# Second block: one run of 24 projection tiles with the spatial gating issued between them

## What is computed

```python
def spatial_gating(u, v, norm_w, ws, bs):
    v = rms_norm(v, norm_w).reshape(B, S // GM_CHUNK, GM_CHUNK, GM_HEADS, GM_HEAD_DIM)
    w = jnp.where(causal, ws, 0.0)
    s = jnp.einsum('hts,bnshd->bnthd', w, v) + bs.T[:, :, None]
    return u * s.reshape(B, S, GM_WIDTH)

def hybrid_mixer(p, ...):                  # p = h @ w_in
    uv = jax.nn.gelu(p[..., COL_GM:COL_Q])
    y_a = spatial_gating(uv[..., :GM_WIDTH], uv[..., GM_WIDTH:], gm_norm_w, gm_ws, gm_bs)
    qkv = jax.nn.silu(short_conv(p[..., COL_Q:COL_Z], conv_w))
    ...                                    # q, k, v, and z = p[..., COL_Z:COL_A]
    o = gated_delta_rule(q, k, v, g, beta)
    y_b = rms_norm(o, o_norm_w) * jax.nn.silu(z)
    return jnp.concatenate([y_a, y_b], axis=-1)
```

## Time and profile before

| | us |
|---|---|
| median of 3 runs | 4131.07 |
| the three runs | 4123.65, 4131.07, 4134.15 |
| span of the profiled execution | 4134.1 |
| gm tiles, from the first matmul | 48.6 |
| gating, no projection tile | 40.3 |
| qkv tiles | 71.7 |
| between qkv and z | 7.0 |
| z tiles | 23.8 |

### The profile page before, as it was taken

The page is one execution under the profiler, slowest core; times in us unless marked ns, Lnnn a source line. Parts: engine busy times, 40 slices in busy tenths (PEclk is TensorE's granted clock), DMA queues, the critical chain, the costliest instruction groups (busy, mean ns, idle before and its releaser), DMA issues. The chain is left out here.

```text
span 4134.1 us, 50723 instructions
## 1 busy us (share of the span) xinstructions
PE 3717.7 (90%) x19009; PEld 3217.5 (78%) x19009; DVE 2578.6 (62%) x4191; ACT 1165.2 (28%) x2042; POOL 338.4 (8%) x281
## 2 busy tenths in 40 slices
PE   8998988899977897989999979999988889689998
PEld 7877755687855796789999979999967758567876
DVE  4556666544645465388999867777754437655544
ACT  1100133211031332133678843333321123412200
POOL 0000010000000020003212322222100000000000
PEclk9999999999989798999999989999999989889999
DMA  4334201232522001158989889999822111022232
GB/s 151 99 105 173 82 11 36 95 95 66 206 75 82 1 1 56 56 176 283 312 290 319 319 310 317 322 320 335 281 82 87 64 36 48 1 82 76 86 107 76
DMA packets 199980, 591.06 MB, mean 143 GB/s; under 512 B 22240, under 2 KB 80480, under 8 KB 197856
## 3 DMA queue, kind: packets, MB, share of 16 engines
q1 hardware_dynamic: 162928, 454.34, 32.8%
q0 software_dynamic: 36864, 134.23, 9.1%
HBM read 536.07 MB, written 52.43 MB: 142 GB/s over the span
## 5 line engine op out<-in xcount | busy, mean ns | idle before, releaser
L615 DVE CAST w_hi<-w_ring 128x1024 fp32r<-128x1024 f32 (+1 forms) x336 | 238.1, 709 | 449.6 <-PE banks L569 402.3
L71 DVE TENSOR_TENSOR w_lo<-w_ring,w_hi 128x1024 fp32r<-128x1024 f32 (+1 forms) x336 | 424.5, 1263 | 11.6
L2753 PE MATMUL out_ps<-w_hi,v_hi 128*128 128x384 f32 x1024 | 349.4, 341 | 41.8 <-DVE w_lo L71 41.8
L569 PE MATMUL banks<-x_hi,w_hi 128*128 128x512 f32 x896 | 355.7, 397 | 29.1 <-DVE x_lo L71 29.1
L2453 PE MATMUL up_ps<-h_hi,u_hi 128*128 128x384 f32 x1024 | 351.2, 343 | 20.2 <-DVE u_lo L71 20.1
L569 PE MATMUL banks<-x_lo,w_hi 128*128 128x512 f32 x896 | 354.3, 395 | 0.0
L569 PE MATMUL banks<-x_hi,w_lo 128*128 128x512 f32 x896 | 353.9, 395 | 0.0
L2753 PE MATMUL out_ps<-w_hi,v_lo 128*128 128x384 f32 x1024 | 347.3, 339 | 0.0
L2753 PE MATMUL out_ps<-w_lo,v_hi 128*128 128x384 f32 x1024 | 347.2, 339 | 0.0
L2453 PE MATMUL up_ps<-h_lo,u_hi 128*128 128x384 f32 x1024 | 343.9, 336 | 0.0
L2453 PE MATMUL up_ps<-h_hi,u_lo 128*128 128x384 f32 x1024 | 343.6, 336 | 0.0
(11 more groups left out here) (563 smaller groups left out, 7705.1 us busy)
## 6 DMA issues: line engine op xcount, KB each, us to landing
expert_tiles<-peer_u SPq DMA_DIRECT2D x128, 512.0 KB, 5.0
expert_tiles<-peer_v SPq DMA_DIRECT2D x128, 512.0 KB, 5.4
w_ring<-w_in SPq DMA_DIRECT2D x104, 512.0 KB, 3.7
w_ring<-ffn_up SPq DMA_DIRECT2D x88, 512.0 KB, 3.6
w_ring<-w_ff SPq DMA_DIRECT2D x64, 512.0 KB, 3.7
ada_ring<-w_ada SPq DMA_DIRECT2D x48, 512.0 KB, 6.4
peer_acts<-act_ring SPq DMA_DIRECT2D x128, 192.0 KB, 5.4
peer_gates<-staging SPq DMA_DIRECT2D x12, 2048.0 KB, 11.1
```

What stands on the lines that cost most here:

```text
L71: return nc.vector.tensor_tensor(self.lo[at], value, self.hi[at].bitcast(F32), ALU.subtract)
L569: last = nc.tensor.matmul(banks[:, j, s, 0:n], a[:, u % 2, k, :], b[:, g * kg + k, x_from + c:x_from + c + n], start=(g == 0 and k == 0 an ...
L615: nc.vector.tensor_copy(w_parts.hi[:, u % 2], ring[:, u % slots]).then_inc(hi_ready, 1)
L2753: last = nc.tensor.matmul(out_ps[:, b, P:T], a[:, n % 2, b * P:b * P + P], r[:, n % 2, :], start=(n == 0 and part == 0), stop=(n == NKEYS ...
```

## The change

A new helper `projections` replaces the three calls of `linear` by one unrolled run of 24 tiles in one block: the same ring, the same split, the same 24 matmuls for a tile, four banks. After each tile it calls `pe_beside`, which puts other TensorE work between tiles; `act_out` and `dve_out` are told the tile's number and put in the gating's ScalarE and VectorE work. The tiles now come in the order v, u, qkv, z (numbers 0 to 3, 4 to 7, 8 to 19, 20 to 23). The four banks that `projections` leaves are one tile `side`, which the front-end norms, the norm of v, the transposes and the mixing matmuls share.

```diff
+def projections(p, x, w, spans, lot, act_out, dve_out, stages, also, banks=None, pe_beside=None):
...
+        @block.tensor
+        def _(pe):
+            for stage in front:
+                stage.tensor(pe)
+            for n in range(nb):
+                pe.wait_ge(w_ready, n + 1)
+                if n >= lot:
+                    pe.wait_ge(bank_free[n % lot], n // lot)
...
+                last.then_inc(units_done, 1)
+                if pe_beside is not None:
+                    pe_beside(pe, n)
...
+            def split(n):
+                dve.wait_ge(landed[n % RING], 16 * (n // RING + 1))
+                if n >= 2:
+                    dve.wait_ge(units_done, n - 1)
...
+            for n in range(nb):
+                if 1 < n + 1 < nb and n:
+                    split(n + 1)
+                dve_out(dve, n, n % lot, psum(n), bank_free[n % lot], units_done)
...
-                linear(p, "gm", d["w_in2"][0:8], DB, 8, h_parts, act_out=copy_out(p, uv, ACT.Gelu_apprx_tanh),
-                       stages=normed_tokens)
...
-                    run(p, [Landed(landed, len(tables)), Norm(p, c3, v, v, 4, T, RMS_EPS, gm_norm, center=False)])
-                spatial_gating(p, uv, mix, v_rows, wT, causal, bs)
...
-                    linear(p, "qkv", d["w_in2"][8:20], DB, 12, h_parts, also={RING - 1: fetch_z},
-                           **short_conv(p, c3, qkv, conv_w, T))
-
-            linear(p, "z", d["w_in2"][20:24], DB, 4, h_parts, act_out=copy_out(p, z, ACT.Silu), before=project_qkv)
...
+        def pe_beside(pe, n):
+            if n == U[0]:
+                for b in range(4):
+                    pe.wait_ge(squared, b + 1)
+                    last = nc.tensor.matmul(side[:, 0, :], p.ones, squares[:, b, :], start=(b == 0), stop=(b == 3))
+                last.then_inc(summed, 1)
+            if n == U[2]:
+                pe.wait_ge(rooted, 1)
+                for b in range(4):
+                    pe.wait_ge(v_scaled, b + 1)
+                    for c in range(NC):
+                        last = nc.tensor.transpose(side[:, b, c * P:c * P + P], v[:, b, c * P:c * P + P], p.ident)
+                    last.then_inc(turned, 1)
+            if n in range(Z[0] - 1, Z[3]):
+                b = n - Z[0] + 1
+                pe.wait_ge(rows_taken, 4)
+                if b >= 2:
+                    pe.wait_ge(biased, 2 * (b - 1))
                 for j in range(2):
+                    for c in range(NC):
+                        last = nc.tensor.matmul(side[:, 2 * (b % 2) + j, c * P:c * P + P], v_rows[:, c, b, :], wT[:, 2 * b + j, :],
+                                                start=True, stop=True)
+                    last.then_inc(mixed, 1)
+
+        def act_out(act, n, j, psum, bank_free):
...
+            if n == V[3]:
+                for b in range(4):
+                    nc.scalar.activation(squares[:, b, :], v[:, b, :], ACT.Square).then_inc(squared, 1)
+            if n == U[0]:
+                act.wait_ge(prepared, 2)
+                act.wait_ge(summed, 1)
+                nc.scalar.activation(rstd[:], side[:, 0, :], ACT.Sqrt, bias=eps_col[:], scale=1.0 / (4 * P)).then_inc(rooted, 1)
+            if n == U[3]:
+                for b in range(4):
+                    act.wait_ge(turned, b + 1)
+                    nc.scalar.activation(v_rows[:, :, b, :], side[:, b, :].rearrange("p (c n) -> p c n", n=P), ACT.Copy) \
+                        .then_inc(rows_taken, 1)
+            if n in QKV:
+                conv.scalar(act, n - QKV[0], psum, bank_free)
...
+        def dve_out(dve, n, j, psum, bank_free, units_done):
...
+            if n == U[0]:
+                dve.wait_ge(rooted, 1)
+                nc.vector.reciprocal(rstd[:], rstd[:]).then_inc(inverted, 1)
+            if n == U[1]:
+                dve.wait_ge(inverted, 1)
+                for b in range(4):
+                    nc.vector.scalar_tensor_tensor(out=v[:, b, :], in0=v[:, b, :], scalar=gm_norm[:, b:b + 1], in1=rstd[:],
+                                                   op0=ALU.mult, op1=ALU.mult).then_inc(v_scaled, 1)
+            if n in QKV:
+                conv.vector(dve, n - QKV[0])
+            if n in Z:
...
+        projections(p, h_parts, d["w_in2"], [(0, T)] * 24, 4, act_out, dve_out, normed_tokens, {}, pe_beside=pe_beside)
```

More of the change, by code:

```diff
@@ L199, in __init__ @@
     def __init__(self, p, ctx, src, dst, kb, width, eps, gain, bias=None, center=True, func=ACT.Identity,
-                 parts=None, first=0, after=None, squares=None, rstd=None, root_in_bank=False, tally=None, lo_ready=None, lo_from=0):
+                 parts=None, first=0, after=None, squares=None, rstd=None, root_in_bank=False, tally=None, lo_ready=None, lo_from=0, sums=None):
         self.p, self.src, self.kb, self.width, self.eps = p, src, kb, width, eps
@@ L211, in __init__ @@
         self.eps_col = p.sb(ctx, "eps_col", [P, 1])
[L212 removed]
+        self.sums = p.ps(ctx, "sums", [P, 2 if center else 1, halves, 512])[:] if sums is None else sums
         if root_in_bank:
@@ L1556, in spatial_gating @@
     with ExitStack() as ctx:
+        h_parts = Parts(p, ctx, "h", [P, DB, T])
+        uv = p.sb(ctx, "uv", [P, 8, T])
         v = uv[:, 4:8, :]
[L1558 to L1571 removed]
+        v_rows = p.sb(ctx, "v_rows", [P, NC, 4, P])
@@ new lines, in project_and_gate @@
+        squares = v_rows[:].rearrange("p c b n -> p (c b n)").rearrange("p (b t) -> p b t", t=T)
+        wT = p.sb(ctx, "wT", [P, GM_HEADS, P])
+        bs = p.sb(ctx, "bs", [P, 4, P])
+        rstd = p.sb(ctx, "v_rstd", [P, T])
+        eps_col = p.sb(ctx, "v_eps", [P, 1])
+        side = p.ps(ctx, "side", [P, 4, T])
+        evicted, prepared, squared, summed, rooted, inverted, v_scaled, turned, rows_taken, mixed, biased, gated = p.sems(
+            ctx, "evicted", "prepared", "squared", "summed", "rooted", "inverted", "v_scaled", "turned", "rows_taken", "mixed",
+            "biased", "gated")
@@ new lines, in project_and_gate, with normed_tokens @@
+        conv = ShortConv(p, ctx, qkv, conv_w, T)
+        tables = (*mixer_tables, (wT[:], d["gm_ws"]), (bs[:], d["gm_bs"]))
+        def normed_tokens(c, banks):
+            for to, source in tables:
+                nc.sync.dma_start(to, source).then_inc(landed, 16)
+            done = Norm(p, c, x, x, DB, T, BETA_LN_EPS / ALPHA ** 2, ln3[:, 0, :], ln3[:, 1, :], tally=sum3,
+                        squares=uv[:, 0:4, :], rstd=rstd[:], sums=side[:, 0:2, :].unsqueeze(2))
+            return [done, Norm(p, c, x, h, DB, T, RMS_EPS, gain, shift, center=False, parts=h_parts, after=done,
+                               squares=uv[:, 4:8, :], sums=side[:, 2:3, :].unsqueeze(2))]
@@ L1579, in _ @@
-            dve.wait_ge(gated, n)
-        @block.tensor
-        def _(pe):
-            pe.wait_ge(masked, 1)
-            for b in range(4):
-                for j in range(2):
-                    for c in range(NC):
-                        last = nc.tensor.matmul(banks[:, j, b, c, :], v_rows[:, c, b, :], wT[:, 2 * b + j, :],
-                                                start=True, stop=True)
-                    last.then_inc(summed, 1)
+                    nc.vector.tensor_tensor(out, side[rows, 2 * (b % 2) + j, :].rearrange("p (c t) -> p c t", t=P),
+                                            over(bs[rows, b:b + 1, :], [64, NC, P]), ALU.add).then_inc(biased, 1)
```

137 lines of the change are left out of this document (96 added, 41 removed).

## The result

The changed kernel took 4090.97 us (median of 4 runs, 4088.87 to 4092.02), the kernel before 4130.74 (4 runs, 4123.65 to 4134.15): a ratio of 0.9901, 95% interval 0.9887 to 0.9915, or 39.8 us less. The forecast was 4092.3.

What follows compares the result with a forecast made beforehand. Program order alone was taken to put the gating on TensorE's path. Removing 142.8 us and putting back 89.8 for tiles and 14.2 for side work saves 38.8: 4131.07 - 38.8 = 4092.3 us, range 4083 to 4105.

Steps and rivals of the forecast that it cites:

- What bounds: Mixer's projections and gating: only program order puts the gating, 40.3 us with TensorE busy for 15.9, on the path.
- The loop: Qkv projection: register addresses make looped tiles take 5.92 us, against 5.62 where the round is written out.
- My bound of 3.6: Upper bound for qkv: 12 tiles at the loop's pace, 0.30 us more each, 3.6 us more in all.
- Rival 1: Qkv stays at 5.92 us a tile because fetches slow it; 3.6 us more, 4095.9 us; chance 0.11.
- The tiles: Projections after the change: twelve qkv tiles 67.4 us and four z tiles 22.4, together 89.8.
- The work between tiles: Gating work on TensorE's path: sums 3.4, stall 1.94, transposes 1.8, mixing 7.0; 14.2 us with a small restart.
- stall: Before tile 6, TensorE waits 1.94 us for the weight split queued on VectorE behind the norm's reciprocal.
- The sum: Whole stage: 142.8 us removed, 89.8 and 14.2 put back, 38.8 us saved; profiled execution 4095.3, median 4092.3.
- rival 2: TensorE's clock drops behind tile 6's stall or in the mixing; 1.8 to 5.1 us more, about 4096; chance 0.13.
- Rivals 3 and 4: Rival 3, and a rival where the low clock holds: 4.7 us more a tile, 4167 us; chance 0.02.
- rival 3: Inserted gating work makes TensorE wait for other engines; half of 24.4 idle us returns, about 4104.5; chance 0.04.
- The test of the other stages: Sign against the forecast: the sum is wrong if another stage of the kernel moves by more than a microsecond.

Runs made afterwards that it cites:

- qkv_unrolled: Kernel before with only the three rounds of the qkv projection loop written out; 4127.70 us, ratio 0.9985 to the kernel before.
- no_gating: Changed kernel with the whole gating left out and half of the mixer's output set to one; 4080.68 us, ratio 0.9861 to the kernel before.
- gating_together: Changed kernel, still one run of 24 tiles, but with the whole gating behind tile 7; 4106.90 us, ratio 0.9925 to the kernel before.
- again: Changed kernel run once more with no edit, to see the spread; 4092.55 us, ratio 0.9887 to the kernel before.
- banks_first: Changed kernel with the four projection PSUM banks allocated ahead of the gating's tile; 4086.62 us, ratio 0.9882 to the kernel before.
- pad32: Changed kernel with 32 bytes left empty ahead of the split weights of the 24 tiles; 4093.03 us, ratio 0.9884 to the kernel before.
- transposes_thrice: Changed kernel with each of the 16 transposes behind tile 6 issued three times; 4102.15 us in one run.

## Why the prediction was right, point by point

**What bounds.** TensorE's order bounded the stage and nothing else took its place: with the gating out of the way TensorE is busy for 67.80 of 67.80 us in the qkv tiles and 29.58 of 29.60 in z. A small wait hides in the busy time: in qkv every second tile comes 0.07 us late.

**The loop.** I read 5.92 against 5.62 as register addresses. `qkv_unrolled` shows it by itself, as the price of the loop: 5.61 a tile, 2.5 us over the qkv tiles. My bound of 3.6 charged all 12 tiles, but only the first 8 are in the loop. Rival 1 falls.

**The tiles.** Forecast 67.4 for qkv and 22.4 for z. Measured 5.62 + 62.18 = 67.8 and 29.60 less four mixings. In `no_gating` tiles lie 5.62 apart (first to last copy of z, 1330.10 to 1346.95, three steps). The term was 0.5 short: 0.4 from every second qkv tile at 5.69 where I had 5.62 for all, and 0.1 from z at 5.62 where I had 5.60.

**The work between tiles.** Forecast 14.2, measured 14.2 with and without the gating. By parts, each against 5.62: sums 9.04 - 5.62 = 3.42 (3.4); stall 7.59 - 5.62 = 1.97 (1.94), of which the hole shows as 1.71; transposes 7.38 - 5.62 = 1.76 (1.8); mixing 4 x 1.78 = 7.1 (7.0). The stall's good fit is luck in part, for two misses cancel in it: split and hand-overs took 1.86 us from the reciprocal's end to TensorE's start where I had 2.09, so the hole is 0.23 shorter than my 1.94, and the start behind the hole costs 0.26 besides where I had 0.1. The lower ends, taken from warm rows, were right in each case where the rows gave two ends.

**The sum.** 191.4 - 153.3 = 38.1 against 38.8. Of the 0.7, 0.5 are the tiles', 0.1 the side work's and 0.1 the first eight tiles', 48.74 (1208.83 to 1264.72 less 3.42, 1.97 and 1.76) against 48.6. That the median of the whole kernel came within 1.3 us of the forecast (4090.97, 4092.3) is luck in part: the profiled execution missed its forecast by 5.1 (4090.2, 4095.3), for reasons outside the stage (below).

**The clock (rival 2).** It stayed at 1.00 after the hole of 1.71 us and through the transposes. The mechanism is real, as the hole of 4.95 us shows, but this stall didn't set it off, and neither did the same hole in the five other kernels that have it (1.69 to 1.74). Of the holes between, the kernel before has one of 1.79 us that kept the clock and one of 3.06, which the prediction left out of its list, behind which the mixing starts at the lower level; its window there:

```profile
1275.20:1278.00 2.80, 2.79 (x13) 2.79 (x14) 0.68 (x1) 0.00 (x0) 0.00 (x0) 0.50 0.00 0
```

The length of a hole doesn't decide by itself, so these numbers give no safe length. Elsewhere in the same trace where the clock was at 1.00 ahead of both, a hole of 2.99 us kept it, and one of 2.51 us behind a dense run of matmuls did not (each hole's end, and the 3.0 us behind it):

```profile
668.77 0.94 PE L1177 MATMUL kv_ps<-v_rows,k_rows 128*128 128x128 f32 x6 [2.99 <-DVE state L1214]
...
2589.39 0.66 PE L2753 MATMUL out_ps<-w_hi,v_hi 128*128 128x384 f32 x1 [2.51 <-DVE w_lo L71]
```

```profile
668.80:671.80 3.00, 3.00 (x27) 3.00 (x28) 2.60 (x9) 0.50 (x1) 0.00 (x0) 1.00 0.02 5
2589.40:2592.40 3.00, 3.00 (x9) 3.00 (x10) 3.00 (x4) 0.86 (x2) 1.01 (x1) 0.50 0.82 304
```

The section of the Trainium skill that the prediction names (TensorE: Matmul & The Clock Gate, HAM oscillation) is about waits of some 3 to 5 us for a transfer between groups of matmuls, behind which the next group starts cold. The hole of 4.95 us agrees with it. The prediction stretched it to a stall of 1.94 us, which is shorter than those waits; that the clock stayed up doesn't speak against the section.

**Rivals 3 and 4.** No wait of TensorE but the priced one, and the clock never fell: both fall. `gating_together` gives what rival 3 was about, waits that the tiles don't cover: 12.25 us, with which the kernel would have stood at about 4103, near rival 3's 4104.5.

**The test of the other stages failed as a test.** I wrote that the sum is wrong if another stage moves by more than a microsecond. By that sign it would be wrong, for other stages did move. The span fell by 43.9 us (4134.1 to 4090.2) and the stage by 38.1. The rest is spread over code that the change doesn't touch: the stage starts 2.7 us later than in the profile of before, from its end to the experts 3.1 us are gone, in the experts 3.2, behind them 2.2. Three of these are not the change's, as far as the profiles go: in `again`, the same kernel, the stage starts within 0.2 us of before's, and the experts differ from the first profile by 3.5 us and what lies behind them by 7.6. The fourth may be in part. From the stage's end to the experts' first matmul the two profiles with the old calls have 369.0 us each, and the twelve with the new run have 365.9 to 368.2. So 1 to 3 us there may come with the change; no run isolates them, and the prediction had nothing for it. The experts show the spread most. First matmul of the experts' up projection and the sums after the experts, in the changed kernel and in `banks_first`, whose stages are equal:

```profile
1727.99 0.69 PE L2611 MATMUL up_ps<-h_hi,u_hi 128*128 128x384 f32 x1 [10.01 <-DVE u_lo L71]
...
2967.26 9.14 PE L349 MATMUL sums<-squares,consts 128*128 128x512 f32 x16 [8.76 <-DVE squares L377]
```

```profile
1727.37 0.69 PE L2612 MATMUL up_ps<-h_hi,u_hi 128*128 128x384 f32 x1 [10.43 <-DVE u_lo L71]
...
2955.30 9.26 PE L349 MATMUL sums<-squares,consts 128*128 128x512 f32 x16 [8.76 <-DVE squares L377]
```

1239.27 us against 1227.93 for the same instructions, 1242.5 in the kernel before (1766.46 to 3008.94) and up to 1247.0 (`pad32`). A stage that differs by 11 us between two profiles can't tell 1 us. The medians hide this: the kernel's 39.8 us agree with 38.1 only within an interval of some 6 us either way. A run's time isn't its span either: in the changed kernel the profiled run took 1.75 us more than its span (4091.95, 4090.2), as in every other kernel here (1.7 to 1.9), so that the match to 0.05 us in the kernel before was probably chance, its profiled execution being another.

## What to carry to other kernels

Small work that has no place of its own in the dependencies can be issued between the tiles of a long projection, and its price is then its warm duration on TensorE, plus what its longest chain exceeds one tile by; put the split of the next tile's weights ahead of the link that waits. Of the gain here two thirds (25.8 of 38.1) came without any interleaving, from keeping the tiles in one run (no hole, cold start or late fetch between them), from writing out the loop, and from a gating without block borders. Judge such a change by its stage in the trace: it repeated to 0.02 us in three profiles (153.29, 153.30 and 153.28 in `banks_first`), so 2 us are plain there, and they are invisible in the whole kernel's time.

## What the runs showed of the hardware that I had not expected

- Transposes by matmul held the granted clock at 1.00 for 5.40 us, behind a stall and a tile (`transposes_thrice`), and 16 of them alone brought it back from 0.50 to 1.00 in the kernel before.
- A hole of 4.95 us cost 1.3 us on top of itself: the first seven matmuls behind it begin at the lower level, 0.43 apart. A hole of 2.99 us kept the clock and one of 2.51 us lost it in the same execution.
- The same fp32r matmul (128x128 by 128x512) runs 0.227, 0.2325 or 0.234 us apart at the same granted clock of 1.00. One cause, the place of the weights, is worth 0.001 to 0.002; the 0.0055 left has no known cause. In qkv a faster pace bought little: in `qkv_unrolled`, at 0.228, two tiles take 11.24 us, in the changed kernel, at 0.234, 11.31, for at the faster pace TensorE waits at every second tile.
- The loop with its addresses in registers cost VectorE 0.22 us over three taps and the stage 0.31 us a tile (5.92 against 5.61).
